# Small fp32 products on TensorE ahead of the three waits of each normalisation, in a two-layer HGRN2 and pooling trunk

## What is computed

```python
def rmsnorm(x, w):
    y = xf * lax.rsqrt(jnp.mean(xf * xf, axis=-1, keepdims=True) + EPS)
    return (y * w).astype(x.dtype)

def ffn_half(h, mod, k0, norm_w, wg, wu, wd):
    u = modulate(rmsnorm(h, norm_w), mod[:, k0, None], mod[:, k0 + 1, None])
    y = (jax.nn.silu(u @ wg) * (u @ wu)) @ wd
    return h + 0.5 * mod[:, k0 + 2, None] * y
...
    return rmsnorm(h, final_norm_w)
```

## Time and profile before

| | us |
|---|---|
| median of the runs | 2028.95 |
| lowest and highest run | 2028.07, 2029.58 |
| span of the profiled execution, first to last instruction | 2028.0 |
| TensorE busy | 1950.9 |
| TensorE weight loads | 1643.0 |
| VectorE busy | 1271.8 |
| ScalarE busy | 794.7 |

### The profile page before, as it was taken

The page is one execution under the profiler, slowest core; times in us unless marked ns, Lnnn a source line. Parts: engine busy times, 40 slices in busy tenths (PEclk is TensorE's granted clock), DMA queues, the critical chain, the costliest instruction groups (busy, mean ns, idle before and its releaser), DMA issues.

```text
span 2028.0 us, 29108 instructions
## 1 busy us (share of the span) xinstructions
PE 1950.9 (96%) x9838; PEld 1643.0 (81%) x9838; DVE 1271.8 (63%) x2059; ACT 794.7 (39%) x1073; POOL 72.4 (4%) x142
## 2 busy tenths in 40 slices
PE   7999999989999999999999989999998999889998
PEld 2888888868887787788888868888886887889997
DVE  3666575657665475657576665756758678465556
ACT  2422322336554323442222344222234576446444
POOL 0000000000000000001000000000000000000000
PEclk8999999989999999999999989999998999999999
DMA  7345454423113243245445424544543333445554
GB/s 303 104 157 185 134 183 159 155 94 104 63 63 110 82 140 119 94 134 205 137 155 177 155 83 146 170 160 142 194 141 114 104 104 110 147 154 168 185 181 150
DMA packets 78661, 287.34 MB, mean 142 GB/s; under 512 B 8768, under 2 KB 10048, under 8 KB 77824
## 3 DMA queue, kind: packets, MB, share of 16 engines
q1 hardware_dynamic: 58912, 212.89, 31.3%
q0 software_dynamic: 19392, 73.34, 10.9%
q10 hardware_dynamic: 288, 0.18, 0.0%
HBM read 285.34 MB, written 1.05 MB: 141 GB/s over the span
## 4 chain that ended last, share of the span: by engine, by line
PE 92%; DVE 3%; DMA 2%; issue 1%; ACT 1%; DVEq 0%; SPq 0%; ACTq 0%
PE bank L327 26%; PE bank L329 26%; PE bank L328 26%; PE bank L441 2%; PE bank L603 1%; DMA raw<-weights 1%; PE bank L489 1%; PE bank L490 1%; PE bank L491 1%; PE bank L368 1%; PE bank L369 1%; PE bank L370 1%; PE bank L560 1%; PE bank L336 1%; PE bank L358 1%
## 5 line engine op out<-in xcount | busy, mean ns | idle before, releaser
L327 PE MATMUL bank<-u_hi,w_hi 128*128 128x512 f32 (+1 forms) x1856 | 676.0, 364 | 0.0
L329 PE MATMUL bank<-u_hi,w_lo 128*128 128x512 f32 (+1 forms) x1856 | 666.3, 359 | 0.0
L328 PE MATMUL bank<-u_lo,w_hi 128*128 128x512 f32 (+1 forms) x1856 | 666.3, 359 | 0.0
L875 DVE TENSOR_TENSOR w_lo<-raw,w_hi 128x1024 fp32r<-128x1024 f32 x384 | 468.9, 1221 | 217.6 <-ACT w_hi L626 189.0
L626 ACT ACTIVATE w_hi<-raw 128x1024 fp32r<-128x1024 f32 x384 | 405.0, 1055 | 491.8 <-DMA raw<-weights 482.2
L329 PEld LDWEIGHTS bank<-u_hi,w_lo 128*128 128x128 f32 x1856 | 350.4, 189 | 52.1
L328 PEld LDWEIGHTS bank<-u_lo,w_hi 128*128 128x128 f32 x1856 | 350.7, 189 | 51.6 <-issue 1.0
L327 PEld LDWEIGHTS bank<-u_hi,w_hi 128*128 128x128 f32 x1856 | 350.7, 189 | 51.5 <-issue 1.0
L327 PE MATMUL bank<-hid_hi,w_hi 128*128 128x512 f32 (+1 forms) x832 | 298.5, 359 | 0.7 <-DVE w_lo L875 0.5
L329 PE MATMUL bank<-hid_hi,w_lo 128*128 128x512 f32 (+1 forms) x832 | 298.2, 358 | 0.0
L328 PE MATMUL bank<-hid_lo,w_hi 128*128 128x512 f32 (+1 forms) x832 | 298.2, 358 | 0.0
(11 more groups left out here) (147 smaller groups left out, 1471.2 us busy)
## 6 DMA issues: line engine op xcount, KB each, us to landing
raw<-weights SPq DMA_DIRECT2D x384, 512.0 KB, 3.5
ada_raw<-adaw POOLq DMA_DIRECT2D x128, 512.0 KB, 4.5
start_w<-weights SPq DMA_DIRECT2D x8, 1024.0 KB, 12.3
box<-box POOLq DMA_DIRECT2D x4, 1024.0 KB, 7.6
h<-resid SPq DMA_DIRECT2D x1, 2048.0 KB, 19.4
silu_c<-c POOLq DMA_DIRECT2D x1, 1024.0 KB, 5.0
out<-sig_a SPq DMA_DIRECT2D x8, 128.0 KB, 2.0
poolw<-poolw POOLq DMA_DIRECT2D x2, 256.0 KB, 9.4
```

The costliest lines, as they stand in the source:

```text
L327: pe.matmul(ps, w_hi[:, slot, k, :], hi(k), start=first, stop=False)
L328: pe.matmul(ps, w_hi[:, slot, k, :], lo(k), start=False, stop=False)
L329: mm = pe.matmul(ps, w_lo[:, slot, k, :], hi(k), start=False, stop=last)
L875: dve.tensor_tensor(view(w_lo, (j % RING) * UNIT, [1, UNIT]), raw[:, j % RING, :], view(w_hi, (j % RING) * UNIT, [1, UNIT]).bitcast(F32), ...
```

## The change

A helper `keep_busy(n, count)` puts `count` fp32 products of the constant tiles `ones` and `ident` (128 columns) into TensorE's queue, for every normalisation but n = 0. Their result goes to bank 7 when n is 2 or 5, else to bank 3. `norm_total` calls it in three places: 12 products ahead of the wait for `s_sqs`, 5 ahead of the wait for `s_diag`, and 10 behind the spreading product, so ahead of the next stage's wait for `u_lo`; the last 10 are left out at n = 6.

```diff
+KEEP_BUSY = (12, 5, 10)
...
+            def keep_busy(n, count):
+
+                if n == 0:
+                    return
+                spare = bank[7] if n % 3 == 2 else bank[3]
+                for _ in range(count):
+                    pe.matmul(spare[:, 0:P], ones[:], ident[:], start=True, stop=True)
+
             def norm_total(n):
                 nt = norm_tok(n)
+                keep_busy(n, KEEP_BUSY[0])
                 pe.wait_ge(s_sqs, (ND + 1) * (n + 1))
                 totals(bank[4], sq_sum, nt).then_inc(s_ssq, 1)
                 if n == 0:
                     start_columns()
 
+                keep_busy(n, KEEP_BUSY[1])
                 pe.wait_ge(s_diag, n + 1)
                 pe.matmul(bank[5][:, 0:nt], ones[:], view(diag, 0, [1, nt]), start=True, stop=True).then_inc(s_bc, 1)
+                if n < 3 * NLAYER:
+                    keep_busy(n, KEEP_BUSY[2])
```

## The result

The changed kernel takes 2015.44 us (median of four runs, 2014.77 to 2016.3) against 2029.26 us before in the same comparison: ratio 0.9934, 95% interval 0.9922 to 0.9946. It is faster by 13.8 us (11.0 to 15.8 us by the interval). The forecast was 2014.6 us. The profiled execution took 2014.77 us, with a span of 2013.1 us. Two executions of the kernel before beside the first group of experiments, at 2781 and 3977 us, were far slower than all others and are left out of every comparison.

What follows compares the result with a forecast made beforehand. TensorE was taken to lose time to waits at normalisations and to 1.2 GHz work behind them. Terms 3.3 + 2.25 + 2.65 + 3.5 + 2.8 - 0.2 = 14.3 us, off 2028.95, gave 2014.6 us; 8-in-10 range 2011 to 2021.

Steps and rivals of the forecast that it cites:

- The clock: At n = 1 to 6, the added products keep TensorE at 2.4 GHz, granted clock 1.00, through the waits.
- The sentence of the Trainium skill: A page saying identity-operand transposes do not bring the array to full clock; given a small chance of applying here.
- the pause at 1707 us: TensorE busy 1.13 of 3.40 us, one idle piece of 2.06 us, clock 1.00 throughout; taken as a survived pause.
- The price of a product and the fit: Each product 0.222 us at 2.4 GHz; 12, 5 and 10 fit waits of 3.01, 1.29 and 2.63 us at n = 1.
- the rivals: Three alternative outcomes for the whole kernel: half the gain (2021.5 us, 0.11), slower (2041 us, 0.08), nothing (2029 us, 0.04).
- the first rival: Half the gain: clock held in some normalisations, lost in others, or DVE or weight splits take some back; 2021.5 us, chance 0.11.
- Normalisation by normalisation: Gains from a faster spreading product and stage start, n = 1 to 6: 3.3, 2.25, 2.65, 3.5, 2.8, -0.2 us.
- the pairs after n = 2 and 3: Stages of six products per k, where DVE comes last: 1.25 and 1.65 us won, besides the spreading product.
- The median: Whole kernel: median 2028.95 us, kept 0.95 us above the profiled span, less 14.3 us gives 2014.6 us.
- The second: Products of constants don't hold the clock and overrun the waits, mostly the third; slower, 2041 us, chance 0.08.
- The third (nothing happens): Added products run faster or are too light, the clock falls as today while they fit; 2029 us, chance 0.04.

Runs made afterwards that it cites:

- the first group of experiments: Four kernels against the changed one: added products with two moving columns, 2038.61 us; counts (12, 0, 0), 2028.6; (12, 5, 0), 2020.67; (0, 5, 10), 2023.14.
- DVE out of the way: Changed kernel, but at n = 2 and 3 DVE makes u_lo for only 32 of each 256 tokens: 2014.37 us, beside 2016.61 for the changed kernel.
- the kernel with the pooling fill: Changed kernel plus 12 (first layer) and 17 (second layer) such products ahead of TensorE's wait for the pooling tables and values: 2015.82 us.
- the two-column products: Changed kernel with the same 152 products in the same places, each with 2 moving columns instead of 128: 2038.61 us.
- the half dose: Changed kernel with 6, 3 and 5 products in the three places instead of 12, 5 and 10: 2023.12 us.
- the 12 and 5 products: Changed kernel without the 10 products of the third place, counts (12, 5, 0): 2020.67 us.

## Why the prediction was right, and where it was off

**The clock (right).** It held at all six normalisations, in both profiled executions of the changed kernel. Constant operands don't matter here: products of `ones` and `ident` hold it. The sentence of the Trainium skill that I had weighed ("TensorE: Matmul & The Clock Gate", Part 4) does not carry over to a product with the identity that sets no transpose mode; the measurement decides, 1.00 against the fall that it would have meant. What was weak is one argument. I took the pause at 1707 us as proof that such a pause is harmless. It was harmless in that execution; in most of the others it wasn't. The margin that I read from it wasn't there. What the runs show is that the clock held wherever the three waits were filled almost whole, and was lost in some normalisations wherever less was filled.

**The price of a product and the fit (right).** 0.222 us forecast, 0.223 measured; 0.17 us of idling is left before the totals at n = 1 where I had 0.34, since twelve products last 2.84 us with the end of the last one, and I had counted 12 x 0.222. The third wait has 0.40 us left, as worked out. Two small sums behind the rivals don't follow from their rows: ten products fit into 2.63 us up to 0.263 us each, not 0.28, and two lost normalisations at 1.8 us each take back 3.6 us, not 2, so the first rival would have stood at about 2023.5 us.

**Normalisation by normalisation.** The distances between instructions of the two profiles give each term. "Won" is the change in the distance from the last real product before the totals to the product with which the stage's slow part ends (the 97th of `natural`, the 49th of `pair`):

| n | forecast us | won us | of it spreading product | of it stage |
|---|---|---|---|---|
| 1 | 3.3 | 3.2 | 0.95 | 2.23 |
| 2 | 2.25 | 1.6 | 0.95 | 0.69 |
| 3 | 2.65 | 2.0 | 0.95 | 1.09 |
| 4 | 3.5 | 3.5 | 0.95 | 2.53 |
| 5 | 2.8 | 2.7 | 0.57 | 2.22 |
| 6 | -0.2 | 0.0 | 0.57 | none |
| sum | 14.3 | 13.0 | | |

The columns don't add up at n = 5 and 6, where the starts of totals, spreading product and stage shift as well. At n = 6 the totals come 0.69 us late (0.7 forecast), and the spreading product takes 0.65 instead of 1.22 us, as forecast; the rest is the second wait, where I had counted 0.1 us lost and 0.13 us are won.

**The mis-sized term: the pairs after n = 2 and 3.** Both are short by the same 0.6 us. I had the right mechanism, DVE sets the pace, and the wrong end. DVE's last two `u_lo` in the changed kernel (one row for both), TensorE's first product of the last but one block, and the first product after the pair:

```profile
818.86 1.67 DVE L972 SCALAR_TENSOR_TENSOR u_lo<-norm_t,shift_c,u_hi 128x256 fp32r<-128x256 f32 x4
...
819.79 0.50 PE L381 MATMUL bank<-u_hi,w_hi 128*128 128x512 f32 x1
...
822.68 0.39 PE L328 MATMUL bank<-u_hi,w_hi 128*128 128x512 f32 x1
```

The row was there before the change: four instructions in one piece, so the last block comes only 0.8 us behind the one before, because no `norm_t` is left to make between them. TensorE needs 1.4 us for a block. It gets block 6 at 819.79 and works through both in 2.89 us; block 7 waits for TensorE, not the reverse. I had counted from the end of that row plus one block. The right count is from the middle of the row plus two: 826.28 + 0.1 + 2.89 = 829.27 against 829.95, 0.7 us, as measured. With DVE out of the way the pair took 11.00 us, which shows the pace but not this detail; the detail is in the rows.

**The median.** 13.0 us are accounted for at the normalisations, 1.3 less than forecast, and 13.8 measured between the medians. That the median came so near the forecast is partly luck: the 0.8 us between the two are within the interval, and no run says where they come from. The two profiles differ by 14.9 us, for a reason that is not the change: n = 0 has no added products, yet its stage was through 2.5 us earlier. 1.0 us of it is an earlier start of the totals, 0.4 go the other way in the pair, and 1.95 are the products of two columns, which ran at another clock, before and after (start, us, instruction):

```profile
38.01 5.69 PE L346 MATMUL bank<-ident,start_rows 2*128 2x2 f32 x32
```

```profile
37.03 3.73 PE L347 MATMUL bank<-ident,start_rows 2*128 2x2 f32 x32
```

From the start of the totals to the spreading product it was 6.60 us before and 4.65 after. In the second profile of the changed kernel it was 4.64 as well, in the kernel with the pooling fill, whose code is the same there, 6.58: it goes by execution. The remaining 0.7 us went the other way, in the second mixer for the most part. I had taken the three runs before, 1.5 us apart, as the scatter; over all groups the kernel before ranged from 2024.6 to 2032.9 us.

**The rivals.** The second is excluded by the clock. Its price was too high: I had 2.0 us lost at each of n = 1 to 4, and the two-column products, ten of which took 4.27 us, cost 0.4 to 1.4 us there and 6.5 us at all six. At n = 1 they delayed the stage by 1.3 us, of which the stage gave back 0.45 (23.66 us instead of 24.11). The third (nothing happens) is excluded. The first, half the gain, did not come true, but the half dose and the 12 and 5 products show that it was near: 2023.1 and 2020.7 us, with the clock lost in some normalisations and held in others.

## What to carry to other kernels

Where TensorE waits a few times for a short chain on other engines, read the granted clock behind the waits: the products after them pay too, here 3.2 us at n = 1 beside 6.8 us of waiting, and 13.8 of 2029 us in all. Filling the waits with products of constants won that back here with full products (those of two columns did harm), with nearly the whole of every wait in the chain filled, and with products that end before the wait does, since those beyond it cost nearly their full 0.22 us each. Then ask at each stage what comes last once TensorE is fast, block by block down to the last one. After n = 2 and 3 it was DVE: the pair at TensorE's own pace (11.0 us) would have won 1.9 and 2.3 us, and won 0.7 and 1.1.

## What was not expected of the hardware

The clock can fall with no pause over 1.51 us, where one-column products lie between the pauses. The same pause, 2.06 us in the same kernel, left the clock at 1.00 in one execution and brought it to 0.50 in another, so a pause that is harmless in one profile is not shown harmless. Where a fall was only put off, the recovery came later too: bridging only the first wait changed nothing (2028.6 us). And fp32 products of two columns were no cheaper than those of 128: five (ten records) took 1.38 us at full clock against 1.36 us.
